# Recurrent heads 1 to 6 in another order, with their gates in three rounded passes

## The reference, cut

```python
z = h @ w_in                                   # g (gate branch) and rec
u = dwconv(rec, conv_w, conv_b, (2, 1))        # 4 taps over tokens
for d, rev in enumerate((False, True)):        # two directions
    r = sigmoid(einsum("bthi,hij->bthj", u, wa[d]) + ba[d])
    i = sigmoid(einsum("bthi,hij->bthj", u, wx[d]) + bx[d])
    log_a = -8 * r * softplus(-lam[d])
    b = sqrt(-expm1(2 * log_a)) * (i * u)
    y += scan(exp(log_a), b, from the context's final state, rev)
out = (gelu(g) * y) @ w_out
```

## Time and profile before

| | us |
|---|---|
| runs, median of 3 (lowest to highest) | 1967.58 (1963.97 to 1968.02) |
| the profiled execution: its time | 1964.01 |
| its span, first to last instruction | 1962.1 |
| busy in the span: TensorE, VectorE, GpSimd, ScalarE | 1924.4, 1664.6, 1276.1, 990.9 |

### The profile page before, as it was taken

One profiled execution on the slowest core, in us unless ns is written; L12 is line 12 of the kernel. 1 busy time (PEld: TensorE's weight loads), 2 busy tenths in 40 slices (PEclk: granted clock), 3 DMA queues, 4 the chain that ended last, 5 costly groups with the idle time before them and its releaser, 6 DMA issues.

```text
span 1962.1 us, 28044 instructions
## 1 busy us (share of the span) xinstructions
PE 1924.4 (98%) x8838; PEld 1570.9 (80%) x8838; DVE 1664.6 (85%) x1752; ACT 990.9 (51%) x1417; POOL 1276.1 (65%) x858
## 2 busy tenths in 40 slices
PE   6999999999999999999999999999999999999999
PEld 3777777788888888888888789878888888888886
DVE  5698889879889989999989886897888888888887
ACT  5867678457444444444444556663334334334334
POOL 4533344566887788887778975475567655656765
PEclk9999999999999999999999999999999999999999
DMA  9223222541223232222332231111111111111114
GB/s 357 100 81 102 98 83 102 199 162 51 90 77 95 86 102 90 89 82 86 96 96 86 97 150 44 65 65 54 54 57 50 64 44 63 54 53 61 49 53 179
DMA packets 78016, 179.74 MB, mean 92 GB/s; under 512 B 5104, under 2 KB 28944, under 8 KB 77328
## 3 DMA queue, kind: packets, MB, share of 16 engines
q1 hardware_dynamic: 77968, 179.13, 26.7%
HBM read 166.52 MB, written 12.58 MB: 91 GB/s over the span
## 4 chain that ended last, share of the span: by engine, by line
PE 84%; DVE 6%; ACT 5%; POOL 2%; issue 2%; DMA 0%; ACTq 0%; DVEq 0%; POOLq 0%
PE ps L1258 41%; PE ps L1278 19%; PE ps L808 15%; PE ps L1063 2%; PE ps L1407 2%; PE ps L870 1%; PE ps L1230 1%; PE ps L1368 1%; DVE rawC L2623 1%; PE ps L941 1%; DVE Y L2545 1%; DVE u L2658 0%; DVE X L2555 0%; PE ps L863 0%; ACT RA L1635 0%
## 5 line engine op out<-in xcount | busy, mean ns | idle before, releaser
L2322 POOL TENSOR_TENSOR So_lo<-So_raw,So_hi 128x512 fp32r<-128x512 f32 x120 | 199.0, 1665 | 199.6 <-DVE So_raw L2965 168.5
L3029 DVE TENSOR_TENSOR Y<-Y,ps 128x1024 f32<-128x1024 f32 x280 | 324.2, 1208 | 3.2
L1837 ACT ACTIVATE So_hi<-So_raw 128x512 fp32r<-128x512 f32 x180 | 112.4, 625 | 145.8 <-POOL So_raw L2314 73.1
L2089 POOL TENSOR_TENSOR red<-red,E_quad 128x512 f32<-128x512 f32 x77 | 124.2, 1613 | 60.9 <-ACT E_quad L1891 58.0
L1837 ACT ACTIVATE WB_hi<-rawB 128x512 fp32r<-128x512 f32 x120 | 74.6, 629 | 165.0 <-PE ps L1258 111.0
L2042 POOL TENSOR_TENSOR WA_lo<-rawA,WA_hi 128x1024 fp32r<-128x1024 f32 x20 | 58.4, 2922 | 126.0 <-DVE u L2658 102.7
L1837 ACT ACTIVATE WA_hi<-rawA 128x512 fp32r<-128x512 f32 x120 | 73.1, 625 | 119.9 <-PE ps L1278 83.3
L1258 PE MATMUL ps<-T_hi,So_hi 128*128 128x512 f32 x336 | 131.2, 391 | 0.0
L1258 PE MATMUL ps<-T_hi,So_lo 128*128 128x512 f32 x336 | 130.8, 389 | 0.0
L1258 PE MATMUL ps<-T_lo,So_hi 128*128 128x512 f32 x336 | 130.7, 389 | 0.0
L1258 PE MATMUL ps<-H_hi,WA_hi 128*128 128x512 f32 x336 | 130.7, 389 | 0.0
(11 more groups left out here) (445 smaller groups left out, 6277.6 us busy)
## 6 DMA issues: line engine op xcount, KB each, us to landing
rawA<-wA SPq DMA_DIRECT2D x62, 512.0 KB, 3.3
rawB<-wB SPq DMA_DIRECT2D x62, 512.0 KB, 3.3
E_quad<-ada SPq DMA_DIRECT2D x44, 512.0 KB, 3.4
quad<-ada SPq DMA_DIRECT2D x8, 2048.0 KB, 9.3
rawB<-wC SPq DMA_DIRECT2D x22, 512.0 KB, 3.8
rawA<-wC SPq DMA_DIRECT2D x20, 512.0 KB, 3.8
ada_first<-ada SPq DMA_DIRECT2D x8, 1024.0 KB, 15.4
outT<-X SPq DMA_DIRECT2D x16, 512.0 KB, 2.7
```

The lines of the kernel that those rows point to most:

```text
L1837: A(dst[:, at:at + HF], op_source(name), ACT.Copy).then_inc(op_hi, 1)
L2089: TT(red[:], red[:], E_quad[:, :, k % 2 * P:k % 2 * P + P], ALU.add).then_inc(red_made, 1)
L2322: TT(lo[:, at:at + HF], op_source(name), hi[:, at:at + HF].bitcast(F32), ALU.subtract)\
L3029: TT(at, at, ps[:, bank:bank + 2, :], ALU.add).then_inc(d_added, 1)
```

## The change

Only heads 1 to 6 change their order; head 0 is followed by the first part of head 1's preparation on ScalarE, head 7 keeps its order but for one rounding of a later weight tile (`round_hi("B", NH + 2)`), which moves ahead of a table load.

- TensorE: unit B(n) comes first, then the column sums, then unit A(n+1) in four pieces (k-tiles 0 to 2, 3 and 4, 5, 6 and 7), with gate 0, 1, 2 and 3 of head n behind each. A gate is three passes over the parts of `gw` and `u`. All gates use banks 3, 4 and 5; each but the first waits until the one before it is evacuated.
- ScalarE: GELU(n) right behind unit B(n), WB, sigmoids, tanh, then rec, first tap and WA of the next head and the high part of `gw`; exp; then the high parts of `u` of the next head (`uc_hi`, `u_hi`); then the roots.
- VectorE: quad(n), convolution of n+1, bias, scans of both directions, combine.
- GpSimd: WA_lo, low part of `gw`, low part of `u` in two pieces, WB_lo, IB*u twice.
- Five buffers are added, placed where nothing else lives at that time; some semaphores are renamed or shared.

```diff
+        u_hi, = overlay(("u_hi", [P, T], F32R))
...
+        gw_hi, gw_lo = overlay(("gw_hi", [P, 4, P], F32R), ("gw_lo", [P, 4, P], F32R))
...
-        rec, u, RA0, Hc_hi, Hc_lo, RA1, IB0, IB1, TH0, TH1, gw = overlay(
-            64, ("rec", [P, TA + 3]), ("u", [P, TA]), ("RA0", [P, TA]), 1.25,
+        u_lo, = overlay(64, ("u_lo", [P, TA + 3], F32R))
+        rec, u, RA0, uc_hi, Hc_hi, Hc_lo, RA1, IB0, IB1, TH0, TH1, gw = overlay(
...
+            def inner_head(hd):
+
+                pe.wait_ge(g_made, hd)
+                unit("B", hd, AB67)
+                pe.wait_ge(gate_evac, 4 * hd)
+                ada_columns(4 * hd, 4, ps[:, 3, 0:4])
+                pe.wait_ge(rec_evac, hd + 1)
+                pe.wait_ge(w_ready["A"], hd + 2)
+
+                def next_unit(ks):
+                    for k in ks:
+                        pieces = [piece(ps[:, 1:3, :], H_hi, H_lo, k, h) for h in range(2)]
+                        pieces.append((ps[:, 0, 0:NC_], Hc_hi[:, k], Hc_lo[:, k]))
+                        mm = product("A", k * P, pieces, k == 0, k == KT - 1)
+                    if KT - 1 in ks:
+                        mm.then_inc(unit_done["A"], 1)
+
+                next_unit((0, 1, 2))
+                pe.wait_ge(operand_ready, hd + 4)
+                pe.wait_ge(rec_parts, hd + 1)
+                pe.wait_ge(ada_added, hd + 1)
+                for gi, ks in enumerate(((3, 4), (5,), (6, 7), ())):
+                    if gi:
+                        pe.wait_ge(gate_evac, 4 * hd + gi)
+                    gate_pieces = [(ps[:, 3, 0:NC_], uc_hi[:], u_lo[:, 2:2 + NC_])]
+                    for h in range(2):
+                        gate_pieces.append((ps[:, 4 + h], u_hi[:, hs(h)],
+                                            u_lo[:, 2 + LAT + h * HF:2 + LAT + h * HF + HF]))
+                    for w, part in ((gw_hi, 0), (gw_hi, 1), (gw_lo, 0)):
+                        for out, hi, lo in gate_pieces:
+                            mm = pe.matmul(out, w[:, gi], (hi, lo)[part], start=w is gw_hi and part == 0,
+                                           stop=w is gw_lo)
+                    mm.then_inc(gate_done, 1)
+                    if ks:
+                        next_unit(ks)
+
             head(0)
             with pe.Fori(1, NH - 1) as hd:
-                head(hd)
+                inner_head(hd)
...
             def head(hd, last=False):
                 first = isinstance(hd, int) and hd == 0
-                act.wait_ge(unit_done["A"], hd + 1)
                 if first:
+                    act.wait_ge(unit_done["A"], 1)
                     A(rec[:, 3 + CUT:2 + TA], ps[:, 2], ACT.Copy).then_inc(rec_evac, 1)
-                else:
-                    act.wait_ge(u_made, hd)
-                    A(rec[:, 2:2 + NC_], ps[:, 0, 0:NC_], ACT.Copy)
-                    A(rec[:, 2 + LAT:2 + TA], flat(ps[:, 1:3, :]), ACT.Copy).then_inc(rec_evac, 1)
-                act.wait_ge(rec_evac, hd + 1)
-                if not first:
-                    act.wait_ge(gate_done, 4 * hd)
-                    act.wait_ge(iu_made, 2 * hd)
-                at = CUT if first else 0
-                A(u[:, at:TA], rec[:, at:TA], ACT.Identity, scale=col("rg_conv_w", hd), bias=col("rg_conv_b", hd))\
-                    .then_inc(conv_step, 1)
-                round_hi("A", hd + 1)
+                    act.wait_ge(rec_evac, 1)
+                    A(u[:, CUT:TA], rec[:, CUT:TA], ACT.Identity, scale=col("rg_conv_w"), bias=col("rg_conv_b"))\
+                        .then_inc(conv_step, 1)
+                    round_hi("A", 1)
...
                 if last:
+                    round_hi("B", NH + 2)
                     act.preload_act_table(ACT.Sqrt)
+
+            def next_tokens(n):
+
+                act.wait_ge(unit_done["A"], n + 1)
+                act.wait_ge(u_made, n)
+                A(rec[:, 2:2 + NC_], ps[:, 0, 0:NC_], ACT.Copy)
+                A(rec[:, 2 + LAT:2 + TA], flat(ps[:, 1:3, :]), ACT.Copy).then_inc(rec_evac, 1)
+                act.wait_ge(rec_evac, n + 1)
+                act.wait_ge(gate_done, 4 * n)
+                act.wait_ge(iu_made, 2 * n)
+                A(u[:], rec[:, 0:TA], ACT.Identity, scale=col("rg_conv_w", n), bias=col("rg_conv_b", n))\
+                    .then_inc(conv_step, 1)
+                round_hi("A", n + 1)
+                act.wait_ge(gw_full, 16 * n + 16)
+                A(gw_hi[:], gw[:], ACT.Copy).then_inc(operand_hi, 1)
+
+            def round_tokens(n):
+
+                act.wait_ge(u_made, n + 1)
+                A(uc_hi[:], u[:, 0:NC_], ACT.Copy)
+                A(u_hi[:], u[:, LAT:TA], ACT.Copy).then_inc(u_parts, 1)
+
+            def inner_head(hd):
+
+                act.preload_act_table(ACT.Gelu_apprx_tanh)
+                act.wait_ge(unit_done["B"], hd + 1)
+                A(Y[:, hd], flat(AB67), ACT.Gelu_apprx_tanh).then_inc(g_made, 1)
+                act.preload_act_table(ACT.Sigmoid)
+                round_hi("B", hd + 1)
+                for gi in range(4):
+                    d = gi // 2
+                    dst, name = ((RA[d], "gate_a_b"), (IB[d], "gate_x_b"))[gi % 2]
+                    act.wait_ge(gate_done, 4 * hd + gi + 1)
+                    act.wait_ge(scan_done, 2 * hd - 1 + d)
+                    A(dst[:, 0:NC_], ps[:, 3, 0:NC_], ACT.Sigmoid, bias=col(name, d * NH + hd))
+                    A(dst[:, LAT:TA], flat(ps[:, 4:6, :]), ACT.Sigmoid, bias=col(name, d * NH + hd))\
+                        .then_inc(gate_evac, 1)
+                for d in range(2):
+                    act.wait_ge(gate_evac, 4 * hd + 2 * d + 2)
+                    act.wait_ge(gy_made, hd)
+                    A(TH[d][:], RA[d][:], ACT.Tanh, scale=s_tanh[:, bass.ds(d * NH + hd, 1)])\
+                        .then_inc(tanh_made, 1)
+                next_tokens(hd + 1)
+                for d in range(2):
+                    A(RA[d][:], RA[d][:], ACT.Exp, scale=s_exp[:, bass.ds(d * NH + hd, 1)]).then_inc(exp_made, 1)
+                act.preload_act_table(ACT.Sqrt)
+                round_tokens(hd + 1)
+                for d in range(2):
+                    act.wait_ge(tanh_made, 2 * hd + d + 1)
+                    A(TH[d][:], TH[d][:], ACT.Sqrt).then_inc(sqrt_made, 1)
 
             act.wait_ge(lam_ready, 1)
             act.wait_ge(memset_done, 5)
             head(0)
+            next_tokens(1)
+            round_tokens(1)
             with act.Fori(1, NH - 1) as hd:
-                head(hd)
+                inner_head(hd)
...
+            def inner_head(hd):
+                lo_of_unit("A", hd + 1)
+                pool.wait_ge(operand_hi, hd + 4)
+                TT(gw_lo[:], gw[:], gw_hi[:].bitcast(F32), ALU.subtract).then_inc(operand_ready, 1)
+                pool.wait_ge(u_parts, hd + 5)
+                TT(u_lo[:, 2:2 + NC_], u[:, 0:NC_], uc_hi[:].bitcast(F32), ALU.subtract)
+                TT(u_lo[:, 2 + LAT:2 + TA], u[:, LAT:TA], u_hi[:].bitcast(F32), ALU.subtract).then_inc(rec_parts, 1)
+                lo_of_unit("B", hd + 1)
+                for d in range(2):
+                    pool.wait_ge(gate_evac, 4 * hd + 2 * d + 2)
+                    TT(IB[d][:], IB[d][:], u[:], ALU.mult).then_inc(iu_made, 1)
+
             with pool.Fori(1, NH - 1) as hd:
-                head(hd)
+                inner_head(hd)
...
+            def inner_head(hd):
+                ada_quad(hd)
+                convolve(hd + 1)
+                add_ada_bias(ps[:, 3, 0:4], ADA0 + 4 * hd, 4, hd + 2)
+                scans(hd, 0)
+                scans(hd, 1)
+                combine(hd)
+
             with dve.Fori(1, NH - 1) as hd:
-                head(hd)
+                inner_head(hd)
```

More of the change, by code:

```diff
@@ L98, in build_trunk @@
             ("WC_lo", [P, D], F32R), ("F_lo", [P, T], F32R), ("F_lo_last", [P, T], F32R))
-        rawC, S1, rawA = sb("rawC", [P, D]), sb("S1", [P, T]), sb("rawA", [P, D])
+        rawC = sb("rawC", [P, D])
+        u_hi, = overlay(("u_hi", [P, T], F32R))
+        S1, rawA = sb("S1", [P, T]), sb("rawA", [P, D])
         Y = sb("Y", [P, KT, T])
@@ L129, in build_trunk @@
         ada_first, = overlay(96 + FR, ("ada_first", [P, 3, 4, D]))
-        rec, u, RA0, Hc_hi, Hc_lo, RA1, IB0, IB1, TH0, TH1, gw = overlay(
-            64, ("rec", [P, TA + 3]), ("u", [P, TA]), ("RA0", [P, TA]), 1.25,
+        u_lo, = overlay(64, ("u_lo", [P, TA + 3], F32R))
+        rec, u, RA0, uc_hi, Hc_hi, Hc_lo, RA1, IB0, IB1, TH0, TH1, gw = overlay(
+            64, ("rec", [P, TA + 3]), ("u", [P, TA]), ("RA0", [P, TA]), ("uc_hi", [P, NC_], F32R), 0.25,
             ("Hc_hi", [P, KT, NC_], F32R), ("Hc_lo", [P, KT, NC_], F32R), ("RA1", [P, TA]),
@@ L844, in first_context @@
             def first_context(g):
-                pe.wait_ge(hc_ready, g + 1)
+                pe.wait_ge(operand_ready, g + 1)
                 for k in (2 * g, 2 * g + 1):
@@ L849, in first_context @@
                 if g == 3:
-                    mm.then_inc(left_rec, 1)
+                    mm.then_inc(rec_parts, 1)
```

(13 more changed lines are left out.)

14 lines of the change are left out of this document (7 added, 7 removed).

## The result

The changed kernel takes **2007.9 us** (median of 4 runs, 2007.4 to 2009.4) against 1967.0 (4 runs, 1964.0 to 1968.0): ratio 1.0216, 95% interval 1.0204 to 1.0228, so slower by 41 us. The forecast was 2010.6. The profiled execution took 2007.95 us (span 2006.2) and began 3.1 us later than that of before: its first gate of head 0 starts at 77.96 instead of 74.85, ahead of anything that the change touches.

What follows compares the result with a forecast made beforehand. TensorE alone was taken to bound each 34.3 us round; the change closes a longer chain through other engines. -1.2 + 5 x 6.9 + 9.3 + 0.4 = +43 on 1964.0, plus 3.6 to the median, gives 2010.6 us, range 1985 to 2032.

Steps and rivals of the forecast that it cites:

- the five rounds: Loop over heads 1 to 6: five rounds each 6.9 us longer, 41.2 against 34.3.
- the tail: Head 7 and projection: evacuations start 3.3 us later, a 2.95 us wait at a projection tile goes; net +0.4.
- TensorE's gain: Loop gates in three passes instead of float32: 7.0 against 8.4 us, saving 1.4 a round, 8 over six.
- Steps 1 to 6: Chain in a round from gate 3's evacuation through ada_quad, convolution, root, both scans, gates 2 and 3: 41.2 us.
- IB*u missing the last scan: Direction 1's scans in a round: IB*u arrives 0.3 later, taking 2.6 us off a round; 1995 us.
- Round 1: First loop round starts from a state of head 0 that is ready early: gains about 1.2 us.
- Head 7: Column sums ahead of unit B(7) need ada_quad(6): 9.3 us idle ahead of that unit, sums included.
- the clock rival: Loop gates run at half clock behind TensorE's waits: 20 us more, 2031; chance 0.12.
- that wait goes: TensorE's 2.95 us wait at the sixth projection tile disappears because the rounding of its weights moves earlier.
- steps 2 to 5: Convolution, roots and scans: VectorE's two-input SBUF operations and GpSimd take turns, waits of 3.0, 1.9, 2.1 and 2.6 us.
- Ports do not matter: GpSimd falls between VectorE's loop operations, so port waits go: rounds of 35.0 us, 1974.6; chance 0.12.
- TensorE stays the bound: Loop chain closes in under 32.9 us: 1956 (faster, 0.04), or 1965 if head 7's wait stays (no change, 0.04).

Runs made afterwards that it cites:

- e9: The changed kernel with float32 gates and no rounding or low parts of u and gw in heads 1 to 6: 1986.9 us, ratio 1.0112.
- e2: The changed kernel with both square roots on ScalarE ahead of the roundings of u: 2005.8 us, ratio 1.0203.
- e3: The changed kernel with two bank sets in turn for the gates' latent columns and a wait for GELU ahead of gate 0: 2006.3 us, ratio 1.0211.
- e4: The changed kernel with WA of the next head rounded ahead of the tanhs, so WA_lo runs beside ada_quad: 1999.0 us, ratio 1.0168.
- e6: The changed kernel with low parts of u and gw cut to one column each, gates reading the high parts instead: 1993.9 us, ratio 1.0142.
- e1: The changed kernel with head 7's column sums behind its unit B instead of ahead: 2008.5 us, ratio 1.0216.
- e10: The changed kernel with the rounding of projection tile 6's weights moved back behind the tail's four copies: 2006.5 us, ratio 1.0206.
- e7: The changed kernel with ten more matmuls of 512 columns ahead of gate 0 in each round, filling TensorE's wait: 2010.8 us, ratio 1.0234.
- e8: The changed kernel with the edits of e1, e2, e3, e4 and e10 together: 2000.4 us, ratio 1.0179.

## Why the prediction was right, and where it was not

The forecast of slower and its mechanism held, and its sum came out 2.7 us above the result. That closeness is partly luck: two terms missed in opposite directions, the five rounds by 5.4 us (29.1 for 34.5) and the tail by 4.9 (5.3 for 0.4).

*TensorE's gain*: there (gate 1 from 238.00 to 239.84, 1.84 at the full clock, for 2.1 as float32), and worth nothing. e9 undoes it, with the roundings that it needs, and is 21 us faster.

*Steps 1 to 6.* Measured from quad(3)'s start: quad done 6.4 (forecast 6.4), convolution 14.0 (14.4), first root 16.6 (17.1), scans of direction 0 24.1 (25.0), of direction 1 34.8 (35.8), next quad 40.2 (41.2). In the round shown each step and each turn is where it was put. Mis-sized: the convolution's turns (2.7 for 3.0) and the turn for u's low part (the operation took 2.92, so it waited 1.4, not 1.9). Over five rounds this is 29.1 for the forecast's 34.5.

*Which of them is first to end.* The steps took one limb as the path. The runs showed a second one close behind, TensorE's queue from gate 0 to gate 3: behind gate 0 it waits only 0.72 and 1.56 us in the round shown. So the prediction's own variant, IB*u missing the last scan and 2.6 off a round, came true in one round of five and took 0.5 off it; the time of 1995 that was drawn from it is out. It does not change the forecast, but it is why e2 and e3 gave nothing like their arithmetic, and why the turn that IB*u missed added so little in e4 and e6.

*Round 1*: -2.0 (forecast -1.2).

*Head 7*: 8.23 idle and 1.7 for the sums at the lower clock, 9.9, where 9.3 was forecast, sums included. As a place it is right; as a cause e1 disproved it.

*The tail*: forecast +0.4 (3.3 less 2.95), measured +5.3. This step failed. Its first half was put at scans that hold up the evacuations of head 7; the gates' piece lost only 0.75 (14.89 for 14.14), because unit B itself had become longer: 15.06 for 11.81, at a mean clock of 0.78. That is the clock rival's mechanism, in a place where it was not looked for, behind the one long wait: 3.25 us with the column sums. As with the wait itself this says where the time stands and not what causes it: in e1 unit B(7) ran at the full clock and nothing was gained. The second half, the wait of 2.95, did go, but the sentence "that wait goes" followed only ScalarE and TensorE. It didn't ask what GpSimd's remainder is then beside, though steps 2 to 5 had asked just that. The last two pieces together lost 2.1 instead of gaining 2.95; by e10, undoing the edit gives back 1.4 at most, and what makes up the rest was not isolated.

*Rivals.* "Ports do not matter" is out (e4, e6, and 5.94 for two taps). The Trainium skill, page "SBUF — State Buffer", section "Who interferes with whom", which says that the operation issued first keeps the port for its length, fits each of these rows; the six `ada_quad` operations at 212.95 kept the 4.71 of the earlier trace rows beside the IB*u of 212.21. "The clock falls too" was right that the stretches come (0.96 in each round) and wrong that they cost in the changed kernel's rounds (e7: nothing, and the one round with the stretch on gate 1 was the shortest); at 2031 it was out of place here, and in place in e8, where it took 1.9 a round. "TensorE stays the bound" is out: it idles 2.56 us in a round ahead of gate 0, 0.5 to 2.1 ahead of gate 1 and, in four rounds of five, 1.56 ahead of gate 3, against 3.5, 2.4 and 1.9 forecast; in all 5 us of a round instead of 8.3, the busy time at the lower clock counted as busy.

Open: no kernel of this order came below 1984.2 us, and the runs don't show one that would reach 1967; why the part behind the norm was 1.4 shorter in the changed kernel's profiled execution was not followed.

## What to carry to other kernels

When work moves to a queue with time to spare, write down what the neighbouring engine does in that moment: here VectorE's busy time rose by 4.0 us in a round though its own work stayed the same, and one moved rounding did the like in the tail. When one wait is removed, follow every instruction that it releases, not only the one that waited. And before trusting the sum of single edits, list all limbs within 1 or 2 us of the longest, each with the clock it will run at: an edit that lengthens a wait can slow the work behind it.
